# The attention's v projected ahead of its q and k in a fused mLSTM and attention block on one core

## What is computed

```python
h = rms_norm(x, mix_norm_g)
proj = h @ w_in            # q_a k_a v_a | q_m k_m v_m o_m | i_m f_m | g_a g_m
y_a = causal attention, 8 heads of 64, with a bias linear in the distance
qk_m = silu(causal_depthwise_conv(concat(q_m, k_m), conv_qk))     # width 4
h_m = mlstm_chunkwise(q_m, k_m, v_m, i_m + b_i, log_sigmoid(f_m + b_f))   # 4 heads of 128
y_m = head_layer_norm(h_m * sigmoid(o_m))
merged = sigmoid(g_a) * (y_a @ w_out_attn) + sigmoid(g_m) * (y_m @ w_out_mlstm)
x = x + merged @ w_o
h = rms_norm(x, ffn_norm_g)
x = x + (silu(h @ w_gate) * (h @ w_up)) @ w_down
return rms_norm(x, final_norm_g)
```

## Time and profile before

| | |
|---|---|
| three timed runs | 390.14 us median (389.74 to 390.36) |
| the profiled execution, its own time | 390.27 us |
| its span in the profile | 388.5 us |
| PE busy | 380.4 us (98%) |
| PEld busy | 324.3 us (83%) |
| DVE busy | 247.9 us (64%) |
| ACT busy | 201.6 us (52%) |
| POOL busy | 34.4 us (9%) |
| DMA read, mean rate | 69.26 MB, 181 GB/s |

### The profile page before, as it was taken

How to read it: one execution, slowest core, us unless ns; L and a number is a source line. 1 busy time by engine, 2 the same in 40 slices (tenths; PEclk the granted TensorE clock), 3 DMA queues, 4 the chain that set the end, 5 groups by cost and what they waited for, 6 DMA issues and landing times.

```text
span 388.5 us, 5183 instructions
## 1 busy us (share of the span) xinstructions
PE 380.4 (98%) x2017; PEld 324.3 (83%) x2017; DVE 247.9 (64%) x329; ACT 201.6 (52%) x249; POOL 34.4 (9%) x39
## 2 busy tenths in 40 slices
PE   8999999999999999999999999999999999999993
PEld 7998888788778888888878888888888888888883
DVE  3989979765366656689747682745738366472325
ACT  3867896564576451743456463461725437163014
POOL 2698010000000000000110000000000000000002
PEclk9999999999999999999999999999999999999998
DMA  7897257937263774466536756639284472930002
GB/s 270 265 304 251 74 185 280 322 115 248 78 210 117 260 249 136 141 202 220 199 108 223 232 184 229 193 132 301 66 281 150 174 250 78 320 108 0 0 2 109
DMA packets 47513, 70.55 MB, mean 182 GB/s; under 512 B 2268, under 2 KB 31240, under 8 KB 47496
## 3 DMA queue, kind: packets, MB, share of 16 engines
q1 hardware_dynamic: 47280, 70.03, 53.7%
q10 hardware_dynamic: 216, 0.28, 0.2%
HBM read 69.26 MB, written 1.05 MB: 181 GB/s over the span
## 4 chain that ended last, share of the span: by engine, by line
PE 97%; issue 1%; DVE 0%; POOL 0%; POOLq 0%; ACT 0%; DVEq 0%; ACTq 0%
PE pa L1194 21%; PE pp L1203 14%; PE pp L1204 13%; PE pp L1205 13%; PE pa L1196 11%; PE pp L1194 4%; PE pp L1181 3%; PE pp L1196 2%; PE pa L1205 2%; PE pa L1203 2%; PE pa L1204 2%; PE pp L1222 2%; PE pa L1484 1%; PE pa L1483 1%; PE pa L1482 1%; PE pa L1300 1%
## 5 line engine op out<-in xcount | busy, mean ns | idle before, releaser
L767 DVE TENSOR_TENSOR w_lo<-w_raw,w_hi 128x2048 fp32r<-128x2048 f32 x38 | 86.4, 2288 | 23.9 <-ACT w_hi L453 23.8
L1194 PE MATMUL pa<-hT,w_hi 128*128 128x512 f32 x352 | 87.9, 392 | 0.0
L453 ACT ACTIVATE w_hi<-w_raw 128x2048 fp32r<-128x2048 f32 x38 | 72.2, 1919 | 19.0 <-DMA w_raw<-in_w_in 9.5
L1194 PEld LDWEIGHTS pa<-hT,w_hi 128*128 128x128 f32 x352 | 63.9, 189 | 11.9
L1130 DVE TENSOR_TENSOR w_lo<-w_raw,w_hi 128x2048 fp32r<-128x2048 f32 x24 | 53.6, 2286 | 8.9 <-ACT w_hi L724 8.9
L1196 PEld LDWEIGHTS pa<-hT,w_lo 128*128 128x128 f32 x352 | 48.0, 190 | 3.4
L1203 PE MATMUL pp<-w_hi,hT 128*128 128x512 f32 x128 | 50.7, 396 | 0.0
L1205 PE MATMUL pp<-w_lo,hT 128*128 128x512 f32 x128 | 49.9, 390 | 0.0
L1204 PE MATMUL pp<-w_hi,hT 128*128 128x512 f32 x128 | 49.9, 390 | 0.0
L1196 PE MATMUL pa<-hT,w_lo 128*128 128x256 f32 x352 | 49.1, 282 | 0.0
L724 ACT ACTIVATE w_hi<-w_raw 128x2048 fp32r<-128x2048 f32 x24 | 44.0, 1898 | 0.0
(11 more groups left out here) (230 smaller groups left out, 459.5 us busy)
## 6 DMA issues: line engine op xcount, KB each, us to landing
w_raw<-in_w_in SPq DMA_DIRECT2D x21, 1024.0 KB, 5.5
w_raw<-in_w_ffn_gate SPq DMA_DIRECT2D x11, 1024.0 KB, 5.3
w_raw<-in_w_ffn_up SPq DMA_DIRECT2D x11, 1024.0 KB, 6.3
w_raw<-in_w_ffn_down SPq DMA_DIRECT2D x11, 1024.0 KB, 6.5
w_raw<-in_w_o SPq DMA_DIRECT2D x4, 1024.0 KB, 5.9
w_raw<-in_w_out_attn SPq DMA_DIRECT2D x2, 1024.0 KB, 5.0
w_raw<-in_w_out_mlstm SPq DMA_DIRECT2D x2, 1024.0 KB, 5.1
x_sb<-in_x SPq DMA_DIRECT2D x2, 512.0 KB, 3.6
```

The source lines that it names most:

```text
L453: nc.scalar.activation(w_hi[:, slot_of(c), :], w_raw[:, c % RAW, :], ACT.Copy).then_inc(hi_ready, 1)
L767: nc.vector.tensor_tensor(w_lo[:, slot_of(c), :], w_raw[:, c % RAW, :], w_hi[:, slot_of(c), :].bitcast(F32), ALU.subtract).then_inc(lo_rea ...
L1194: mm(banks[:, f, :], w_hi[:, s, w[k]], hT[:, k], start=(k == 0), stop=False)
```

## The change

The order of the blocks becomes Q_M, K_M, V_A, Q_A, K_A, V_M, O_M, gates: the attention's v is projected as chunks 4 and 5 into banks pp 0 and 1. Of Q_A and K_A the first half goes to pp 2 and 3 and the second to pp 0 and 1. The attention bursts lie behind chunks 11, 13, 15, 17 and 19. The columns of i and exp(-m) come from fp32r products of the split rows with columns of the selection matrix, those of exp(-m) only behind chunk 11, and exp(-m) is computed behind the eight exponentials. pv writes each token half apart, so three products for each head. The 36-row transpose that gives vcol moves from PE's start into chunk 0. The square of the last quarter of x2 is computed by DVE.

```diff
-FEATURE_MAJOR = 4
+BLOCKS = [Q_M, K_M, V_A, Q_A, K_A, V_M, O_M, G_A, G_A + 512, G_M, G_M + 512]
+SPLIT = (1, 3, 4)
+TOKEN_MAJOR = (2, 5, 6, 7, 8, 9, 10)
...
         gate_rest = sem("gate_rest")
@@ -283,7 +301,7 @@
 
             if c < C_OUT:
                 b, h = divmod(c, 2)
-                if 0 < b < FEATURE_MAJOR:
+                if b in SPLIT:
                     return w_in_k[:, :, BLOCKS[b] + 256 * h:BLOCKS[b] + 256 * (h + 1)]
...
+                                         scale=0.0).then_inc(sel_r_set, 1)
+                    nc.scalar.activation(e_rows, sel[:, 0:S], ACT.Copy, scale=0.0).then_inc(sel_r_set, 1)
                 if c == 3:
 
                     act.wait_ge(scans_done, 1)
+                    act.wait_ge(sel_r_set, 3)
                     nc.scalar.activation(m_rows[0:H_M, :], row_m, ACT.Copy).then_inc(mrow_hi_set, 1)
-                    nc.scalar.activation(row_e, row_e, ACT.Exp, scale=-1.0).then_inc(exp_m_done, 1)
+                    nc.scalar.activation(i_rows[0:H_M, :], row_i, ACT.Copy).then_inc(irow_hi_set, 1)
                     tap3(2)
                 if c in (4, 5):
...
-                if c == 12:
+                if c == 14:
                     copy_pT(0)
                     copy_pT(1)
-                if c == 14:
-                    ya_hi_first()
-                    softmax_exp(2)
                 if c == 15:
                     read_block(6, lambda t: o_t[:, t], ACT.Sigmoid)
                 if c == 16:
+                    act.wait_ge(pv_done, 2)
+                    softmax_exp(2)
+                    softmax_exp(3)
+                if c == 18:
                     copy_pT(2)
-                    softmax_exp(3)
-                    act.wait_ge(pv_done, 2)
-                if c == 18:
-                    ya_hi(2)
                     copy_pT(3)
                 if c == 20:
-                    ya_hi(3)
+                    ya_hi_second()
                 if c == 3:
                     tap3(3)
-                    copy_rest(4)
                 elif c == 5:
+                    read_block(2, lambda t: va[:, t], ACT.Copy)
+                elif c == 6:
                     copy_rest(6)
+                elif c == 7:
+                    copy_rest(7)
+                elif c == 8:
+                    copy_rest(8)
                 split_hi(c + AHEAD)
...
-                elif c == 4:
-                    copy_rest(5)
                 elif c == 7:
-                    copy_rest(7)
+                    act.wait_ge(exp_m_done, 1)
+                    nc.scalar.activation(e_rows[0:H_M, :], row_e, ACT.Copy).then_inc(erow_hi_set, 1)
                 elif c == 9:
-                    read_block(4, lambda t: va[:, t], ACT.Copy)
+                    copy_rest(9)
...
-            square(3, 1, x2_ready, 4)
+            act.wait_ge(x2_ready, 4)
+            act.wait_ge(sumsq_done, 3)
+            nc.scalar.activation(o_sb[:, 0:D // 4], x_t[:, 1, QUARTERS[2]], ACT.Square, scale=D ** -0.5,
+                                 accum_out=sumsq[:, 7:8]).then_inc(sumsq_done, 1)
...
-                dve.wait_ge(qk_rest, c - 3)
-                ft = 4 * (b - 2) + 2 * h
-                nc.vector.tensor_tensor(qk_a[:, ft:ft + 2, :], pp[:, 2 * h:2 * h + 2, 0:S], qk_a[:, ft:ft + 2, :],
-                                        ALU.add).then_inc(proj_free[h], 1)
+                dve.wait_ge(qk_rest, c - 5)
+                ft = 4 * (b - 3) + 2 * h
+                nc.vector.tensor_tensor(qk_a[:, ft:ft + 2, :], pp[:, 2 - 2 * h:4 - 2 * h, 0:S], qk_a[:, ft:ft + 2, :],
+                                        ALU.add).then_inc(proj_free[1 - h], 1)
...
+            def ya_first():
+                dve.wait_ge(pv_done, 2)
+                pair = yT_hi[:, 0:2, :].rearrange("p f (t n) -> p (f t) n", t=T)
+                nc.vector.tensor_copy(pair, va_first).then_inc(ya_hi_set, 2)
                 dve.wait_ge(ya_hi_set, 2)
-                nc.vector.tensor_tensor(yT_lo[:, 0:2, :], pa[:, 0, :].rearrange("p (f n) -> p f n", f=2),
-                                        yT_hi[:, 0:2, :].bitcast(F32), ALU.subtract).then_inc(ya_lo_set, 2)
+                nc.vector.tensor_tensor(yT_lo[:, 0:2, :].rearrange("p f (t n) -> p (f t) n", t=T), va_first,
+                                        pair.bitcast(F32), ALU.subtract).then_inc(ya_lo_set, 2)
...
+                dve.wait_ge(num_done, 1 if h == 0 else H_M)
...
                     dve.wait_ge(mrow_hi_set, 1)
-                    dve.wait_ge(sel_r_set, 2)
+                    dve.wait_ge(sel_r_set, 3)
                     nc.vector.tensor_tensor(m_rows[32:32 + H_M, :], row_m, m_rows[0:H_M, :].bitcast(F32),
                                             ALU.subtract).then_inc(mrow_lo_set, 1)
+                    dve.wait_ge(irow_hi_set, 1)
+                    nc.vector.tensor_tensor(i_rows[32:32 + H_M, :], row_i, i_rows[0:H_M, :].bitcast(F32),
+                                            ALU.subtract).then_inc(irow_lo_set, 1)
                     k_in_sum(0)
                     k_in_sum(1)
-                if c == 4:
-                    qk_sum(5)
-                elif c == 5:
+                if c == 6:
                     qk_sum(6)
+                elif c == 7:
+                    qk_sum(7)
                 if c == 8:
                     for h in range(H_M):
                         score_w(h)
-                if c == 10:
-                    score_max(0)
-                    score_max(1)
-                if c == 11:
-                    prob_scale(0)
-                    prob_scale(1)
+                    dve.wait_ge(erow_hi_set, 1)
+                    nc.vector.tensor_tensor(e_rows[32:32 + H_M, :], row_e, e_rows[0:H_M, :].bitcast(F32),
+                                            ALU.subtract).then_inc(erow_lo_set, 1)
                 if c == 12:
 
                     dve.wait_ge(cols_turned, 1)
...
+                if c == 12:
+                    score_max(0)
+                    score_max(1)
+                    dve.wait_ge(e_cols_turned, 1)
+                    nc.vector.tensor_scalar(rcol[:, 8:16], pa[:, 0, 384:392], -1.0, None, ALU.mult
+                                            ).then_inc(rcol_set, 1)
+                if c == 13:
+                    prob_scale(0)
+                    prob_scale(1)
+                if c == 16:
+                    dve.wait_ge(scores_done, H_A)
                     score_max(2)
-                if c == 15:
+                    score_max(3)
+                    ya_first()
+                if c == 17:
                     prob_scale(2)
-                if c == 16:
-                    score_max(3)
-                if c == 17:
                     prob_scale(3)
-                if c == 18:
-                    ya_lo(2)
+                if c == 20:
+                    ya_lo_second()
                     head_out(0)
-                if c == 20:
-                    ya_lo(3)
-                    for h in range(1, H_M):
-                        head_out(h)
+                    head_out(1)
+                    head_out(2)
+                    head_out(3)
...
+                    nc.vector.tensor_scalar(rcol[:, 0:8], pa[:, 0, 0:8], -1.0, None, ALU.mult).then_inc(rcol_set, 1)
...
+                elif c == 8:
+                    qk_sum(8)
+                elif c == 9:
+                    qk_sum(9)
...
+            dve.wait_ge(x2_ready, 4)
+            dve.wait_ge(sumsq_done, 3)
+            nc.vector.tensor_tensor_reduce(
+                out=o_sb[:, 512:512 + D // 4], in0=x_t[:, 1, QUARTERS[3]], in1=x_t[:, 1, QUARTERS[3]], scale=1.0 / D,
+                scalar=sumsq[:, 6:7], op0=ALU.mult, op1=ALU.add, accum_out=meansq[:, 3:4]).then_inc(x2_rest_square, 1)
+            dve.wait_ge(x2_rest_square, 1)
+            dve.wait_ge(sumsq_done, 4)
+            nc.vector.scalar_tensor_tensor(out=meansq[:, 3:4], in0=sumsq[:, 7:8], scalar=EPS, in1=meansq[:, 3:4],
+                                           op0=ALU.add, op1=ALU.add).then_inc(x2_meansq_set, 1)
...
-                    if c == 6 and f == 1:
-                        pe.wait_ge(rcol_set, 1)
...
-            pe.wait_ge(vec_loaded, 32)
-            nc.tensor.transpose(pp[:, 1, S:S + 36], vec_rows, ident[0:36, 0:36]).then_inc(vec_turned, 1)
...
-                pe.wait_ge(exp_m_done, 1)
-                pe.wait_ge(proj_free[0], 1)
-                for n, row in enumerate((row_i, row_e)):
-                    for t in range(T):
-                        ins = nc.tensor.transpose(pp[:, 1, 8 * n + 4 * t:8 * n + 4 * t + 4],
-                                                  row[:, t * P:(t + 1) * P], ident[0:H_M, 0:H_M])
+                pe.wait_ge(irow_lo_set, 1)
+                for t in range(T):
+                    ins = mm(pa[:, 0, 4 * t:4 * t + 4], i_rows[:, t * P:(t + 1) * P], sel_cols, start=True, stop=True)
                 ins.then_inc(cols_turned, 1)
+
+            def denominator_columns():
+
+                pe.wait_ge(w_ready, H_M)
+                pe.wait_ge(erow_lo_set, 1)
```

(97 more changed lines are left out.)

63 lines of the change are left out of this document (34 added, 29 removed).

## The result

The changed kernel takes 397.03 us (median of six runs, 395.19 to 397.88) against 390.16 of the kernel before: ratio 1.0177, 95% interval 1.0159 to 1.0194, so 1.8% slower. The forecast was 393.5 us with a range to 395.9: the sign was right, the size was half of what came (3.4 against 6.9 us). The profiled run has a span of 395.1 us (before 388.5) and a time of 396.83.

A forecast was written before the change was run, and what follows sets the result against it. TensorE, busy 380.4 of 388.5 us, was taken to bound the kernel. Terms 3.6 + 0.3 + 0.05 - 0.4 + 0.05 - 0.3 = +3.3 on 390.27, less 0.1, gave 393.5 us; range 392.2 to 395.9.

The forecast's parts named there:

- chunk 7 starts later: At chunk 7, TensorE waits 4.3 us for ACT's two copies of V_A; the chunk starts 3.55 us later than before.
- chunk 7 itself: Chunk 7's first products run slower behind a drained TensorE, costing 0.05 us.
- chunks 8 and 9 feature-major: Chunks 8 and 9 give back the 0.3 us that TensorE is earlier up to chunk 6.
- chunk 10's wait: Before chunk 10, the wait for its bank, emptied last by qk_sum(8), costs 0 to 0.4 us, taken as +0.05.
- bursts, with pv: Bursts from chunk 9 to 19: one fewer saves 0.7, denominator_columns cost 0.2, eight more pv products 0.1; -0.4 us.
- turns behind chunk 17: At prob_turn(3), DVE's chain from the scores and TensorE's arrival tie at 11.7 us; 0 to 0.3, taken as +0.05.
- second norm: At the second normed block's transposes, 0.35 us of stall shrinks with a shorter norm chain; -0.3 us.
- three signs: Wrong if TensorE waits under 3 us at chunk 7, its clock falls, or it waits over 0.5 us later.
- Rival A: In the gap at chunk 7 TensorE's clock halves, losing 1.5 to 3 us; 395 to 396.5 us, chance 0.18.
- Rival C: In the attention bursts, pv's products run one after the other: +2.6 us, 396.1 us; chance 0.04.
- Rival B: At chunk 7, the copies of V_A don't hold TensorE up: -1.1 us, 389.1 us; chance 0.06.
- the heads and SP's queue: Four head_out behind chunk 19, about 11 us in all, hidden by products; SP's loads wait for the same bursts as before.

The follow-up runs named there:

- e1: The changed kernel with ACT's two copies of V_A ahead of the eight exponentials instead of behind them; 390.71 us, ratio to the kernel before 1.0029.
- e3: As e2, with pv of the third and fourth pair written with two products for each head again; 389.57 us, ratio 0.9995.
- e4: The changed kernel with ACT's copies of V_A in the middle of the exponentials, behind those of two heads; 394.74 us.
- e2: As e1, with ACT's wait for pv of the first two pairs behind the third and fourth pair's exponentials; 389.92 us, ratio 0.9999.
- e5: As e3, with copy_rest(6) and qk_sum(6) in round 5 of ACT and DVE instead of round 6; 388.88 us, ratio 0.9975.
- e10: The changed kernel with ACT's copies of V_A one step later, behind the split of chunk 9; 398.13 us.
- e6: The kernel before with only a quarter of the squares of x2 moved to DVE, as the change does; 389.60 us, ratio 0.9987.
- e7: The kernel before with only the 36-row transpose for vcol moved into chunk 0; 389.62 us, ratio 0.9999.
- e9: The kernel before with each pv half's first product split in two, 24 products instead of 16; 390.62 us, ratio 1.0012.

## Why the prediction came out wrong in size

The terms, forecast and as the profile after gives them, from starts of the same work in both traces:

| step | forecast | measured |
|---|---|---|
| chunk 7 starts later | +3.55 | +2.34 (53.44 to 55.78) |
| chunk 7 itself | +0.05 | +2.7 (5.64 to 8.35) |
| chunks 8 and 9 feature-major | +0.3 | +0.3 |
| chunk 10's wait | +0.05 | 0 |
| bursts, with pv | -0.4 | about 0 |
| turns behind chunk 17 | +0.05 | +1.34 |
| second norm | -0.3 | -0.3 |
| sum | +3.3 | +6.4; the span grew by 6.6, the median by 6.9 |

Two of the three signs that the prediction named for being wrong came: the clock fell, and PE waited for 0.7 us behind chunk 7, at the turns.

**The stop at chunk 7** was right in place and cause, and e1 shows that it is this and nothing else. It was forecast 1.2 us too late, because ACT got to tap3 at 41.70, not at 43.0. The reason is in the trace of before and I did not see it: the first instruction of the scans on DVE took 1.34 us there, with POOL's selection on the mask running beside it until 38.1; after the change it took 0.40, with POOL done at 36.85. That is 0.94 of the 1.3 us; the rest is the few tenths that the prediction added to the 42.75 of before. Before, DVE and POOL:

```profile
37.00 1.34 DVE L982 SCALAR_TENSOR_TENSOR o_sb<-o_sb 4x256 f32<-4x256 f32 x1
```

```profile
35.92 2.15 POOL L411 TENSOR_SCALAR_AFFINE_SELECT alibi<-alibi 128x1024 bf16<-128x1024 bf16 x2
```

After, DVE and POOL:

```profile
36.99 0.40 DVE L1009 SCALAR_TENSOR_TENSOR o_sb<-o_sb 4x256 f32<-4x256 f32 x1
```

```profile
34.70 2.15 POOL L429 TENSOR_SCALAR_AFFINE_SELECT alibi<-alibi 128x1024 bf16<-128x1024 bf16 x2
```

e1, e3 and e4 have the long form as well, each with POOL still at work when the instruction starts, and e2 and e5 to e10 the short one, with POOL done: twelve profiles without an exception, but no run that moves POOL's work by intent. With the short form the old order of chunks too has tap3 early, at 41.54 to 41.85 (e6, e7, e9). So it is a matter of the run and not of the change, and the earlier trace rows stood on an unlucky one.

**The clock** is the step that failed. The sum holds +0.05 for chunk 7 itself, that is, a full clock behind the stop; measured are +2.7, with the granted clock at half for 6.8 us. Rival A had the mechanism and, with 1.5 to 3 us, about the right price, but a chance of only 0.18. That chance rested on one row: clock still full over 4.4 us with PE nearly idle. The row is one outcome and no bound. In the profiles a stop of 3.2 us was enough, and the fall came 2.2 us into it; over all runs of the changed kernel it came each time. The rule of the Trainium skill (TensorE: Matmul & The Clock Gate, section Why this matters for your kernels), cited with rival A, had warned of it: it sets the limit for idle gaps at about 3 us. The trace of before seemed to disagree. The stops of 3.2 and 4.6 us agree with the page; e4's profiled run fell with a stop of 2.3 us, which is shorter than its limit, and there the measurement decides. With the measured 2.7 in the sum the forecast would have been 396.2.

**The turns behind chunk 17.** The prediction called it a tie at +0.05; measured are 1.34. It reckoned with 11.45 us for the chain from maxima to scaled rows. That length came from the first pair of the kernel before, where the exponential table was already loaded. Behind read_block(6), a sigmoid, it is not, and the change puts the load behind the wait. e2 shows the load's place as the cause: with the wait moved, the load is early and the stop is gone.

**The bursts.** The saving on entries, exits and switches came about as forecast. That is worked out and not seen in one line: from the end of chunk 9 to the start of chunk 20 the kernel before takes 67.2 us and the changed one 68.7, 1.34 of them the stop, so the bursts as a whole cost the same within 0.2 us. denominator_columns cost 0.22 as forecast, and what is left for the saving is 0.5 to 0.7. The mis-sized term is pv, forecast at 0.1 for eight more products; e3 and e9 show 0.06 each, 0.5 in all, where 0.1 was put down. Rival C, that the halves lose their overlap, would have been 2.6, and didn't happen: the four pv are still made in pairs side by side.

**Rival B**, no stop, can be read from e1 to e5: it would have given not 389.1 but 390.7, and 389.9 with the table load also out of the way. The missing part is the pv products and, in runs such as e1's profile, the wait for qk_sum(6), for which the prediction has no term; behind the stop it doesn't show. Chunk 10 didn't wait, and the heads and SP's queue were hidden as said.

## What to carry to other kernels

When a block is moved ahead in a schedule that keeps the matrix engine full, look first at who empties its banks and what stands ahead of that on that engine's queue: here two copies of 1.0 us together, behind the wrong neighbours, cost 6.3 us. A stop of the matrix engine of 1 to 5 us is to be priced with the loss of its clock behind it, and not by one trace in which the clock held. A second wait added ahead of an activation whose table isn't loaded can hold up the load too, so put it behind the activation, as e2 did.

## What the runs showed of the hardware that was not expected

The clock fell in 1 of 6 runs of the kernel whose profile has a stop of 1.1 us, in 4 of 6 for 2.3 us, and in all for 3.2 and 4.6 us, while it held for 4.4 us of near idleness at the end of the kernel before. Once down, it stayed at half for 6.8 us in the profiles of the changed kernel and of e10 and for 3.4 us in that of e4. In e4's profile PE was at work again, for 0.2 us, when it fell.

A 4x256 instruction on DVE takes 0.40 us or 1.35 us, the longer whenever POOL's masking of the 128x1024 bf16 tile was still running at its start, and it then ended 0.26 us after POOL did (38.34 and 38.07 us in the kernel before; the same in e1, e3 and e4). The convolution's instructions beside the same POOL work don't wait; they read one tensor from PSUM (region_a<-pp,vcol,region_a), where this one reads both from SBUF. No run separates that from other causes.

Splitting an fp32 product on 64 columns of the array, with the same columns streamed, costs about 0.06 us for each product more (e3, e9).
